# A state-space layer whose decay factors come from rows of running sums, carried across the partitions by transfers, in place of products with a triangle

## The reference, cut to what matters

```python
proj = h @ w_in                                   # 1024 -> z 2048, xBC 4096, dt 32
xbc = silu(causal_depthwise_conv(xbc, conv_w, conv_b))
dt = softplus(dt + dt_bias);  a = -exp(a_log)
# for each chunk of 128 tokens:
acs = cumsum(dtc * a, axis=1)                     # running sums, one per head
decay = exp(where(mask, acs[:, :, None] - acs[:, None, :], -inf))
cb = einsum("blgn,bsgn->blsg", cc, bc)
y_diag = einsum("blsg,blsgr,bsgrp->blgrp", cb, decay, xdt)
y_off = einsum("blgn,bgrpn->blgrp", cc, state) * exp(acs)[..., None]
decay_to_end = exp(acs[:, -1:] - acs)
# after the chunks: y + d_skip * x, times silu(z), RMS norm by group, times norm_w, @ w_out
```

## Time and profile before

| what | value |
|---|---|
| median of 3 runs | 1307.31 us (1304.4 to 1308.39) |
| the profiled execution | 1304.56 us, span 1302.8 us |
| granted TensorE clock, mean | 0.997 |
| PE busy | 1278.1 us, 98% |
| DVE, ACT, POOL busy | 766.1, 684.0, 121.5 us |
| HBM read over the span | 217.87 MB |
| the state-space layer | about 195 to 426 us of the span; slots 12 to 20 lie in 289.4 to 374.2 us |

### The profile page before, as it was taken

The page is one execution under the profiler, slowest core; times in us unless marked ns, Lnnn a source line. Parts: engine busy times, 40 slices in busy tenths (PEclk is TensorE's granted clock), DMA queues, the critical chain, the costliest instruction groups (busy, mean ns, idle before and its releaser), DMA issues.

```text
span 1302.8 us, 18348 instructions
## 1 busy us (share of the span) xinstructions
PE 1278.1 (98%) x6934; PEld 1094.7 (84%) x6934; DVE 766.1 (59%) x908; ACT 684.0 (53%) x940; POOL 121.5 (9%) x198
## 2 busy tenths in 40 slices
PE   8999999999999999999999999989999999999997
PEld 7888889999788888888888888877888888999896
DVE  5655645778786555544555545775555554666654
ACT  6554435578884544443544434854644543444554
POOL 3000000007730000000000000620000000000000
PEclk9999999999999999999999999999999999999999
DMA  9655645443237555565555563412565565564431
GB/s 299 210 178 208 221 139 194 156 168 98 97 106 250 161 192 179 177 221 166 179 176 176 179 226 124 162 38 93 194 193 181 196 215 164 148 190 185 145 115 49
DMA packets 180654, 219.81 MB, mean 169 GB/s; under 512 B 8714, under 2 KB 132943, under 8 KB 180591
## 3 DMA queue, kind: packets, MB, share of 16 engines
q1 hardware_dynamic: 179614, 218.01, 50.6%
q10 hardware_dynamic: 688, 0.79, 0.2%
q0 software_dynamic: 288, 0.15, 0.0%
HBM read 217.87 MB, written 1.05 MB: 168 GB/s over the span
## 4 chain that ended last, share of the span: by engine, by line
PE 88%; DVE 5%; ACT 4%; issue 1%; DMA 1%; SPq 1%; POOL 0%; DVEq 0%; POOLq 0%; ACTq 0%
PE acc L612 27%; PE acc L614 27%; PE acc L613 27%; PE tr L629 4%; DVE w_lo L1952 1%; ACT w_hi L1351 1%; PE tr L921 1%; DMA raw<-in_ffn_w_up 1%; PE aux L1059 1%; PE acc L1040 1%; ACT xT_hi L1364 0%; ACT R_hi L1562 0%; ACT junk L1418 0%; SPq L474 0%; ACT junk L1599 0%
## 5 line engine op out<-in xcount | busy, mean ns | idle before, releaser
L1952 DVE TENSOR_TENSOR w_lo<-raw,w_hi 128x2048 fp32r<-128x2048 f32 (+1 forms) x195 | 438.3, 2275 | 178.3 <-ACT w_hi L1351 178.1
L1351 ACT ACTIVATE w_hi<-raw 128x2048 fp32r<-128x2048 f32 (+1 forms) x197 | 367.3, 1900 | 118.8 <-PE acc L614 118.1
L612 PE MATMUL acc<-w_hi,xT_hi 128*128 128x512 f32 (+1 forms) x914 | 362.2, 396 | 0.6 <-DVE w_lo L2570 0.4
L614 PE MATMUL acc<-w_hi,xT_lo 128*128 128x512 f32 (+1 forms) x914 | 355.0, 388 | 0.0
L613 PE MATMUL acc<-w_lo,xT_hi 128*128 128x512 f32 (+1 forms) x914 | 354.2, 388 | 0.0
L614 PEld LDWEIGHTS acc<-w_hi,xT_lo 128*128 128x128 f32 x914 | 171.6, 188 | 36.2
L612 PEld LDWEIGHTS acc<-w_hi,xT_hi 128*128 128x128 f32 x914 | 171.8, 188 | 35.6 <-issue 1.4
L613 PEld LDWEIGHTS acc<-w_lo,xT_hi 128*128 128x128 f32 x914 | 172.0, 188 | 32.9
L612 PE MATMUL acc<-w_hi,hT_hi 128*128 128x512 f32 x448 | 175.8, 392 | 0.3 <-DVE y_sb L2470 0.3
L614 PE MATMUL acc<-w_hi,hT_lo 128*128 128x512 f32 x448 | 174.5, 389 | 0.0
L613 PE MATMUL acc<-w_lo,hT_hi 128*128 128x512 f32 x448 | 174.4, 389 | 0.0
(11 more groups left out here) (298 smaller groups left out, 1131.2 us busy)
## 6 DMA issues: line engine op xcount, KB each, us to landing
raw<-in_ffn_w_down SPq DMA_DIRECT2D x88, 512.0 KB, 4.9
raw<-in_ffn_w_gate SPq DMA_DIRECT2D x86, 512.0 KB, 4.3
raw<-in_ffn_w_up SPq DMA_DIRECT2D x86, 512.0 KB, 5.3
raw<-in_ssm_w_in SPq DMA_DIRECT2D x48, 512.0 KB, 4.6
raw<-in_w_in_a SPq DMA_DIRECT2D x64, 256.0 KB, 4.0
raw<-in_ssm_w_out SPq DMA_DIRECT2D x16, 512.0 KB, 4.4
raw<-in_mla_w_out SPq DMA_DIRECT2D x8, 512.0 KB, 4.4
raw<-in_w_out_a SPq DMA_DIRECT2D x8, 512.0 KB, 4.7
```

The lines of the kernel that those rows point to most:

```text
L612: pe.matmul(o, lh, rh, start=start, stop=False, skip_group_check=skip)
L614: return pe.matmul(o, ll, rh, start=False, stop=stop, skip_group_check=skip)
L1351: inst = act.activation(w_hi[:, u % RING, 0:n], raw[:, u % RING, 0:n], ACT.Copy)
L1952: inst = dve.tensor_tensor(w_lo[:, u % RING, 0:n], raw[:, u % RING, 0:n], w_hi[:, u % RING, 0:n].bitcast(F32), ALU.subtract)
```

## The change

The running sums are now made once for all heads, and the differences of running sums that the decay needs are taken by subtraction:

- At n = 8 PE makes the running sums of both chunks with tokens on partitions (64 columns instead of 32) and, in two more products, with heads on partitions (32 rows of 256). ACT copies the first to `acs`, the second to `dtT`, and stores dtT in a new 32 KB buffer in DRAM, `decay_rows`, from its own queue.
- For each group ACT then starts a transfer (`sum_rows`) that reads four rows (4 KB) and writes them to all 128 partitions of one of three buffers E[g % 3], 512 KB written. Groups 0 and 1 are started in pair 5, group g + 2 in slot 12 + g, where ACT for g > 0 first waits until y(g - 1) is made.
- POOL subtracts the token's own sum and takes the minimum with 0 (`segments(g)`): eight instructions of 128 x 128 a group, in place. It does group 0 ahead of slot 11, group 1 behind its slot 12, and group n - 11 behind slot n up to 18.
- ACT takes the exponential in place, second chunk first; DVE multiplies as before, second chunk first.
- The triangle products, `high_factors`, R_hi, R_lo, dA_hi, dA_lo and the matrix `after_r` go.
- "g" moves: g(0) into the middle of unit 21, g(1), g(2), g(3) ahead of output units 1, 2 and 4. hT_hi and hT_lo are one instruction a block instead of four, and ssm_norm_w is applied where the output weights are split: two instructions of 1024 columns in place of one of 2048, on ACT and on DVE.
- square_gated(1) moves on ACT from the end of pair 8 to behind slot 18; gated_norm(0), (1), (2) on POOL move from slots 17, 18, 20 to 18, 19, 20, behind `segments`. On DVE g(1) goes ahead of scale_gated(3). Some splits stand elsewhere on ACT in pair 10.

```diff
@@ mamba_slots
+    if n >= 21:
+        found.append(("g", n - 21))
     if 12 <= n < 14 + G:
         found.append(("cb", n - 12))
-    for name, first in (("y", 13), ("seg", 12), ("state", 13)):
+    for name, first in (("y", 13), ("decay", 12), ("state", 13)):
...
-    if n >= 20:
-        found.append(("g", n - 20))
@@ PE, small
-                            pe.matmul(tr[:, k % 2, 0:NH], upto[:], dA[:, 1, :], start=True, stop=True)\
-                                .then_inc(turned, 1)
+                            pe.matmul(tr[:, k % 2, 0:TB * NH], upto[:], dA[:].rearrange("p b n -> p (b n)"),
+                                      start=True, stop=True)
+                            for tb in range(TB):
+                                last = pe.matmul(tr[0:NH, k % 2, (tb + 1) * P:(tb + 2) * P], dA[:, tb, :], upto[:],
+                                                 start=True, stop=True)
...
-                        elif name == "seg":
-                            for tb in range(TB):
-                                pe.wait_ge(r_hi_ready, 2 * g + tb + 1)
-                                pe.wait_ge(r_ready, 2 * g + tb + 1)
-                                if g:
-                                    pe.wait_ge(exp_done, 2 * g + tb - 1)
-                                pe.matmul(aux[:, tb, :], after_r[:], R_hi[:, tb, :], start=True, stop=False)
-                                pe.matmul(aux[:, tb, :], after_r[:], R_lo[:, tb, :], start=False, stop=True)\
-                                    .then_inc(seg_ready, 1)
@@ PE, pairs and gated_ready
+                        elif (s, half) == (10, 1):
+                            token_unit(c.unit, c.pair, 4, 2, KD, 512, done=False)
+                            small(21, "g")
+                            token_unit(c.unit, c.pair, 6, 2, KD, 512, at=FIRST)
...
-                    if n in (1, 3):
-                        small(22 + n // 2)
+                    if n in (1, 2, 4):
+                        small(22 + (1, 2, 4).index(n))
@@ ACT
+                def sum_rows(g):
+                    act.dma_start(E[:, g % 3, :, :].rearrange("p r t -> p (r t)"),
+                                  across(decay_rows[R * g:R * g + R, :].rearrange("r t -> (r t)"), R * T))\
+                        .then_inc(sums_landed[g % 3], 16)
...
+                            act.dma_start(decay_rows[:, :], dtT[0:NH, :]).then_inc(sums_stored, 16)
...
+                        elif name == "decay":
+                            if g + 2 < G:
+                                if g:
+                                    act.wait_ge(turned, ky[0] + 1)
+                                sum_rows(g + 2)
+                            act.wait_ge(seg_ready, 2 * g + 2)
+                            read = note(act.activation(dend[:, g % 2, :], E[:, g % 3, :, P - 1], ACT.Exp))
+                            for tb in (1, 0):
+                                if tb == 0:
+                                    act.wait_ge(act_chain, read)
+                                e = E[:, g % 3, :, tb * P:(tb + 1) * P]
+                                act.activation(e, e, ACT.Exp).then_inc(exp_done, 1)
...
-                def high_factors(g):
...
+                    if s == 9:
+                        square_gated(1)
...
+                    if s == 5:
+                        act.wait_ge(sums_stored, 16)
+                        sum_rows(0)
+                        sum_rows(1)
@@ POOL
+                def segments(g):
+                    pool.wait_ge(sums_landed[g % 3], 16 * (g // 3 + 1))
+                    for tb in range(TB):
+                        for r in range(R):
+                            e = E[:, g % 3, r, tb * P:(tb + 1) * P]
+                            inst = pool.tensor_scalar(e, e, acs[:, tb, R * g + r:R * g + r + 1], 0.0,
+                                                      ALU.subtract, ALU.min)
+                        inst.then_inc(seg_ready, 1)
...
                 for n in range(22):
+                    if n == 11:
+                        turn_done(pool, acs_turn[0])
+                        segments(0)
                     small(n)
-                    if n in (17, 18, 20):
-                        gated_norm((n - 16) // 2)
+                    if 12 <= n < 11 + G:
+                        segments(n - 11)
+                    if n >= 18 and n < 21:
+                        gated_norm(n - 18)
@@ split of the output weights (ACT; DVE alike with scalar_tensor_tensor)
+                    for a, b, n in norm:
+                        inst = act.activation(w_hi[:, u % RING, a:b], raw[:, u % RING, a:b], ACT.Copy, scale=col(n))
```

More of the change, by code:

```diff
@@ L93, in weight_norm, with first @@
 def weight_norm(u):
-    n = u - sum(len(UNITS_OF[name.rstrip("0123")]) for name in PHASES[:-1])
-    return None if not 0 <= n < 8 else (NORM_KV, NORM_B)[n // 4] + 4 * (n % 2)
+    def first(name):
+        return sum(len(UNITS_OF[before.rstrip("0123")]) for before in PHASES[:PHASES.index(name)])
+    n = u - first("stick")
+    if 0 <= n < 8:
+        return [(512 * k, 512 * k + 512, (NORM_KV, NORM_B)[n // 4] + 4 * (n % 2) + k) for k in range(4)]
+    n = u - first("mamba") - 25
+    if 0 <= n < 8:
+        return [(D * k, D * k + D, SSM_NORM + 2 * n + k) for k in range(2)]
+    return None
 def unscaled(name):
     return name[:3] == "ffn" or name == "mla"
-MAMBA_TURNS = {"dt": 1, "acs": 1, "btok": 1, "xs": TB, "cb": 1, "y": 2, "seg": 0, "state": 0, "g": TB}
+MAMBA_TURNS = {"dt": 1, "acs": 1, "btok": 1, "xs": TB, "cb": 1, "y": 2, "decay": 0, "state": 0, "g": TB}
 SMALLS = 16 * 9
@@ L353, in program @@
         dt_act = sem("dt_act")
-        r_ready = sem("r_ready")
-        r_hi_ready = sem("r_hi_ready")
+        sums_copied = sem("sums_copied")
+        sums_stored = sem("sums_stored")
+        sums_landed = [sem(f"sums_landed{n}") for n in range(3)]
         seg_ready = sem("seg_ready")
@@ L865, in mamba, with small @@
                 c.pair += 2
-                def small(n):
+                def small(n, only=None):
                     for name, g in mamba_slots(n):
+                        if only and name != only:
+                            continue
                         k = c.turn
@@ L1352, in split @@
                 else:
-                    for k in range(4):
-                        at = slice(512 * k, 512 * k + 512)
-                        inst = act.activation(w_hi[:, u % RING, at], raw[:, u % RING, at], ACT.Copy, scale=col(norm + k))
+                    for a, b, n in norm:
+                        inst = act.activation(w_hi[:, u % RING, a:b], raw[:, u % RING, a:b], ACT.Copy, scale=col(n))
                 inst.then_inc(hi_ready, 1)
@@ L1624, in mamba @@
                 u = c.unit
-                split_to(u + 3)
                 small(22)
@@ L1629, in mamba @@
                 split_to(u + 7)
+                small(24)
                 sums(DI // P)
@@ L1954, in split @@
                 else:
-                    for k in range(4):
-                        at = slice(512 * k, 512 * k + 512)
-                        inst = dve.scalar_tensor_tensor(w_lo[:, u % RING, at], raw[:, u % RING, at], col(norm + k),
-                                                        w_hi[:, u % RING, at].bitcast(F32), ALU.mult, ALU.subtract)
+                    for a, b, n in norm:
+                        inst = dve.scalar_tensor_tensor(w_lo[:, u % RING, a:b], raw[:, u % RING, a:b], col(n),
+                                                        w_hi[:, u % RING, a:b].bitcast(F32), ALU.mult, ALU.subtract)
                 inst.then_inc(lo_ready, 1)
```

124 lines of the change are left out of this document (53 added, 71 removed).

## The result

The changed kernel takes 1312.89 us (median of 6 runs, 1311.72 to 1315.19), the kernel before on the same chip 1307.53 (6 runs, 1304.4 to 1308.39): a ratio of 1.0048, 95% interval 1.0036 to 1.0059. It is slower by 5.4 us, and outside the range. The profiled execution took 1311.72, with a span of 1310.0 against 1302.8 before.

What follows compares the result with a forecast made beforehand. The prediction took PE's stream, busy 98% of the span, as the bound. Its terms, -8.1 + 0.5 - 4.15 + 1.5 = -10.25 us, set on a mean of 1306.2, gave 1296 us, range 1291.5 to 1302 (8 in 10).

Steps and rivals of the forecast that it cites:

- rival B: Slots 13 to 19: POOL's eight short instructions, blocked by DVE or slow, take 11.4 us a group; 1316 us, chance 0.08.
- 8 x 0.35 = 2.8 us: POOL's eight subtractions a group cost 0.35 us each, 2.8 against 2.0 before; undisturbed bounds 1.5 and 4.9.
- Room 8.2 us for segments: Between the rows' landing and y(g + 1), POOL has 8.2 us for segments, so up to 6.5 us is hidden.
- The blocking: DVE instructions with two SBUF inputs and POOL ones reading SBUF exclude each other; segments takes up to 6.5 us.
- The triangle products: Eight groups of products leave PE's stream, 1.01 us each, 8.1 us less; new running-sum products add 0.5.
- Waits that go: PE's waits at slot 18 (2.35 us), slot 20 (0.8) and the first output unit (1.0) go: 4.15 us.
- New waits in slots 18 to 20: gated_norm(0) behind segments(7) delays DVE and y(6): 1.5 us of new waits together, bounds 0 and 6.
- Transfers: Eight row transfers of 512 KB, each landing in 6.6 us, 4 MB in all, are no bound.

Runs made afterwards that it cites:

- e2: Changed kernel with each of POOL's eight subtractions a group doing only 64 of its 128 columns, the rest left out: 1299.63 us, one run.
- e6: Changed kernel with POOL's eight instructions a group replaced by four two-input ones of 512 columns (subtract, then multiply by the triangle): 1306.72 us.
- e5: Complete changed kernel with the subtraction shared: POOL does four instructions a group for the first chunk, ACT four for the second: 1294.11 us.
- e10: Changed kernel with DVE's w_lo for eleven weight units replaced by a one-input multiplication by 0, issued twice in a row: 1311.62 us.
- e11: The kernel of e5 with gated_norm(0) put back ahead of segments(7) on POOL: 1295.42 us.
- e8: The tail alone: kernel before with only the edits behind the decay factors (g moved, gains merged, squares and gated_norm moved); triangle products stay: 1300.33 us.
- e1: Changed kernel with POOL's eight subtractions a group replaced by two additions of 512 columns, sign and minimum left out: 1294.64 us.
- e7: Changed kernel with 11, 16 and 8 unread products on PE filling its waits for y(1), y(4) and y(6): 1312.34 us.
- e3: Changed kernel with POOL's eight instructions a group doing only the minimum, the subtraction left out: 1305.28 us, one run.
- e4: Changed kernel with all eight differences a group on ACT, as relu(sum - row), in place of POOL; nothing left out: 1300.04 us.
- e9: Changed kernel with DVE's w_lo for eleven weight units replaced by a one-input multiplication by 0, issued once: 1302.6 us.

## Why the prediction was wrong

The direction was wrong. What happened is rival B's outcome, slower because of POOL, but not by its sum: it wanted 11.4 us a group to reach 1316 and 9.9 to equal the kernel before, and a group of subtractions took 6.8 with all its standing, which B's own room of 8.2 would have hidden. B named the right engine with the same wrong threshold. By the steps:

- **"8 x 0.35 = 2.8 us"**: it was 0.69 to 0.71 each (rows of L2706), 5.5 a group back to back, above my undisturbed bound of 4.9 too. I had set it between a one-column row and a two-input row and gone to the lower because it has one input. e2 shows how it splits: 0.28 us whatever the width, 3.3 ns a column.
- **"Room 8.2 us for segments"**: this is the step that failed. A right duration alone would not have saved the forecast. The measured 6.8 us a group, standing included, is under 8.2, so by this step it costs nothing. Even 5.5 with all of the blocking that I had allowed, 5.5 + 2.3 + 1.4 = 9.2, makes the slots 1.0 us longer, 7 in all: 1303, still faster than before. I had worked the room out as a latency: from the landing of a group's rows to the y that needs them, two slots later. But one POOL serves every slot, and what it can give each is PE's slot less its other work. By the runs that is 9.2 us less 3.1 of xdt, ys and xdtd and less some 3.1 of standing for DVE (between 279 and 375 us the changed kernel's group instructions are busy for 93.0 us in eight groups, and undisturbed they would be 64 x 0.69 + 40 x 0.61 = 68.6): 3.0 us, and the line of the table begins at 3.3. The same sum gives a standing of 3.1 a group in e6 and 2.8 in e5. A buffer that is three groups deep lets the transfers be early; it doesn't give the engine more hours.
- **The blocking** was in the text but only in the upper bound of segments, not on xdt, ys and xdtd, where it falls as often (3.65 for 0.61). Its mechanism as I cited it was the narrower half. What e10 shows is that a one-input tensor_scalar of 2048 columns on DVE shuts POOL out as well. The Trainium skill ("SBUF — State Buffer", Who interferes with whom) says both: two inputs in SBUF contend with GpSimd's reads, and tensor_scalar can enter a mode that takes the shared pair for the whole instruction. The trace agrees with each (four columns 2.34 us beside a two-input w_lo of 2.29, in e11; xdt 1.67 beside a one-input one of 1.23, in e10). And the products with the accumulator beside which segments ran (L2241, six from 299.60 and six from 302.54) left it at 0.69 us each: these, which read the accumulator in PSUM, didn't disturb it.
- **The triangle products**, 8.1 us less 0.5: right. In the changed kernel the state product follows y at once. In e5 and e8 a y product with what follows to the next unit takes 2.03 and 2.96 us (335.54 to 337.57; 339.35 to 342.30), so 0.93 a group, 7.4 in all against my 8.1. The running sums' products took 0.82 us in place of 0.14 (265.74 to 266.56; before 266.15 to 266.29), 0.7 against my 0.5.
- **Waits that go**, 4.15: right in all three places. Slot 18's turned columns take 1.29 us in the changed kernel, slot 20 has none, the first output unit 5.68:

```profile
356.70 1.04 PE L638 MATMUL tr<-ident,xsT 128*128 128x128 f32 x8
357.99 0.70 PE L912 MATMUL tr<-state,CT 128*128 128x256 f32 x2 [0.25 <-ACT ys L1553]
...
389.32 0.59 PE L621 MATMUL acc<-w_hi,hT_hi 128*128 128x512 f32 x1
...
395.00 0.38 PE L638 MATMUL tr<-ident,ys 128*128 128x128 f32 x2
```

- **New waits in slots 18 to 20**, 1.5: 1.2 us in e5 (0.15 ahead of y(6) and 1.05 behind it), by the way I had drawn: gated_norm(0), DVE's scaling, the E products, the split, and then cbm, which PE waited for. In e1, where segments is shorter still, there is none in these slots. In the changed kernel it is 1.9 + 0.8.
- **Transfers**: right. They land in 4.9 us, and POOL waits for them only ahead of the first group.

```profile
E<-decay_rows ACTq DMA_DIRECT2D x8, 512.0 KB, 4.9
```

The bill of the changed kernel against e5, 17.0 us up to the first output unit (389.32 against 372.33): longer gaps ahead of y(1), y(4), y(6), 2.7 + 3.9 + 1.9 = 8.5; the y products of the first two, 3.04 and 3.44 for 1.73, 3.0; the units behind the three, 1.6 + 1.3 + 1.6 = 4.5: 16.0. About half stands as waits and half as slow products; e7 shows that the two trade against each other, as far as it kept the clock up. e5, which keeps all of the change and gives half of POOL's part to ACT, measures 1294.1 against the 1296 forecast. By the spans of the two profiled executions it is 1302.8 - 1292.4 = 10.4 us faster, and the terms as measured are -7.4 + 0.7 - 4.15 + 1.2 = -9.7, against -10.25 in the sum: the rest of the sum held term by term.

What stays open: the exact size of the standing (about 3 us a group) isn't fixed by a run of its own; it shifts with what DVE has beside POOL. And by medians the tail alone gave 6.6 us where the trace accounts for 3.4 to 3.9; the profiled execution of before lies 2.75 us below its median, which covers most of it, and no run looks at why.

## What to carry to other kernels

Before work is moved to an engine that looks idle, add up its whole period there: own work, new work, and the time it will stand for a neighbour, against the period of the engine that leads, slot by slot. Depth of buffers and earliness of transfers buy latency, never throughput. And price a short instruction by an instruction of its kind and width, or by its fixed part first: eight of 128 columns cost 5.5 us where two of 512 cost 2.1; if the trace has none, an estimate "between two rows" should carry its upper end into the forecast when the threshold lies near it.

## What the runs showed of the hardware

- GpSimd's tensor_scalar with a column as operand: 0.50 us for 64 columns (e2), 0.71 for 128 (changed), 0.60 for 128 with one operation instead of two (e3). A two-input subtraction of 512 columns with a broadcast operand: 1.04 us; the multiplication with the triangle 1.30 (both e6).
- ScalarE does the same 128 columns (relu with a column as bias) every 0.30 us when eight stand in a row (2.43 for 8, e4; a single row reads 0.39, as they overlap), less than half of GpSimd's 0.69 from start to start.
- DVE and GpSimd took turns by whole instructions: four columns on GpSimd, 0.20 us by themselves (e5), took 2.34 us beside a DVE instruction of 2.29 that had begun 0.01 us earlier (e11).
- After PE had stood for 2.5 and 3.7 us in the changed kernel, the granted clock was 0.56 and 0.50 (the lower of its two levels, 1.2 of 2.4 GHz) in the y product and 0.76 and 0.80 in the unit behind it: y products took 3.0 and 3.4 us instead of 1.73, units 7.6 and 7.0 instead of 5.9 and 5.7. With the pause filled by other products it stayed at 1.00 (311 to 320 us of e7).
- The fall can come late: behind y(4) of e9, where PE had stood 2.8 us, and behind y(6) of the changed kernel (1.9 us ahead of it and 0.8 after it) the y product still ran at 1.00, and the unit after it at 0.77 (7.3 us each).
